# Gate and up projections by seven block products (Strassen's form) in a two-layer streaming encoder trunk on Trainium2

## The reference

```python
D_MODEL = 1024; SEQ = 512; DEC_SEQ = 32; DEPTH = 2; D_FF = 2816

def rms_norm(x, w):
    xf = x.astype(F32)
    y = xf * lax.rsqrt(jnp.mean(xf * xf, axis=-1, keepdims=True) + EPS)
    return (y * w.astype(F32)).astype(x.dtype)

def swiglu(x, w_gu, w_down):
    gate, up = jnp.split(x @ w_gu, 2, axis=-1)
    return (jax.nn.silu(gate) * up) @ w_down

# in trunk(), for every layer l:
    h = h + 0.5 * swiglu(rms_norm(h, p['norm_ffn1'][l]), p['ffn1_w_gu'][l], p['ffn1_w_down'][l])
    ...                                     # mixer
    h = h + 0.5 * swiglu(rms_norm(h, p['norm_ffn2'][l]), p['ffn2_w_gu'][l], p['ffn2_w_down'][l])
```

## Time and profile before

| | us |
|---|---|
| median of 3 runs | 2420.63 |
| lowest, highest | 2418.0, 2421.4 |
| span of the profiled execution | 2420.0 |
| PE busy in it | 2389.0 |
| PEld busy | 2266.8 |
| DVE busy | 1428.3 |
| ACT busy | 940.4 |

### The profile page before, as it was taken

How to read it: one execution, slowest core, us unless ns; L and a number is a source line. 1 busy time by engine, 2 the same in 40 slices (tenths; PEclk the granted TensorE clock), 3 DMA queues, 4 the chain that set the end, 5 groups by cost and what they waited for, 6 DMA issues and landing times.

```text
span 2420.0 us, 48986 instructions
## 1 busy us (share of the span) xinstructions
PE 2389.0 (99%) x19329; PEld 2266.8 (94%) x19329; DVE 1428.3 (59%) x2253; ACT 940.4 (39%) x1369; POOL 13.9 (1%) x50
## 2 busy tenths in 40 slices
PE   9999999999999999999999999999999999999998
PEld 8999999998999999999999999999999989999997
DVE  6553555788577555534555553555788866543554
ACT  4221233576355442222233221224677744221232
POOL 1000000000000000000000000000000000000000
PEclk9999999999999999999999999999999999999999
DMA  5232232332422233322332232332222222232231
GB/s 143 87 109 66 87 100 70 106 115 73 124 69 67 66 94 89 104 79 78 91 91 79 87 111 67 92 92 84 67 77 66 65 72 87 87 113 61 87 102 49
DMA packets 396031, 208.77 MB, mean 86 GB/s; under 512 B 10015, under 2 KB 392086, under 8 KB 395894
## 3 DMA queue, kind: packets, MB, share of 16 engines
q1 hardware_dynamic: 390502, 203.17, 29.2%
q10 hardware_dynamic: 5392, 3.72, 0.5%
HBM read 201.41 MB, written 5.45 MB: 85 GB/s over the span
## 4 chain that ended last, share of the span: by engine, by line
PE 84%; DVE 7%; ACT 4%; DVEq 3%; issue 1%; ACTq 1%; DMA 0%; SPq 0%
PE PD L2054 20%; PE PD L2050 14%; PE PD L2060 14%; PE PD L2061 14%; PE PD L2062 12%; PE PD L2059 2%; PE PD L2056 2%; DVE wlo L1216 1%; DVE c_xl L1745 1%; DVE c_xl L1721 1%; DVEq L1723 1%; DVEq L1731 1%; DVEq L1746 1%; ACT whi L538 0%; PE PM L2467 0%
## 5 line engine op out<-in xcount | busy, mean ns | idle before, releaser
L538 ACT ACTIVATE whi<-raw 128x1024 fp32r<-128x1024 f32 (+4 forms) x348 | 381.2, 1096 | 938.3 <-PE PD L2062 932.6
L2050 PE MATMUL PD<-XB,whi 128*128 128x288 f32 x2008 | 602.6, 300 | 0.4 <-DVE wlo L1216 0.4
L2061 PE MATMUL PD<-XB,wlo 128*128 128x288 f32 x2008 | 591.9, 295 | 0.0
L2060 PE MATMUL PD<-XB,whi 128*128 128x288 f32 x2008 | 591.3, 294 | 0.0
L2062 PE MATMUL PD<-XB,wlo 128*128 128x256 f32 x2008 | 558.8, 278 | 0.0
L2054 PE MATMUL PD<-XB,whi 128*128 128x512 f32 x1392 | 551.5, 396 | 0.5 <-DVE XB L1254 0.5
L2061 PEld LDWEIGHTS PD<-XB,wlo 128*128 128x128 f32 x2008 | 377.7, 188 | 63.8
L2050 PEld LDWEIGHTS PD<-XB,whi 128*128 128x128 f32 x2008 | 376.7, 188 | 3.4 <-DVE wlo L1216 0.8
L2062 PEld LDWEIGHTS PD<-XB,wlo 128*128 128x128 f32 x2008 | 377.8, 188 | 0.0
L2060 PEld LDWEIGHTS PD<-XB,whi 128*128 128x128 f32 x2008 | 377.7, 188 | 0.0
L2054 PE MATMUL PD<-AB,whi 128*128 128x512 f32 x704 | 277.9, 395 | 0.0
(11 more groups left out here) (444 smaller groups left out, 3433.7 us busy)
## 6 DMA issues: line engine op xcount, KB each, us to landing
raw<-in_ffn_w_gu SPq DMA_DIRECT2D x176, 512.0 KB, 3.8
raw<-in_ffn_w_down SPq DMA_DIRECT2D x32, 768.0 KB, 4.8
raw<-in_ab_w_in SPq DMA_DIRECT2D x44, 512.0 KB, 3.9
raw<-in_ffn_w_down SPq DMA_DIRECT2D x32, 640.0 KB, 4.4
raw<-in_c_w_in SPq DMA_DIRECT2D x32, 512.0 KB, 4.1
LM<-cum_rows SPq DMA_DIRECT2D x8, 512.0 KB, 4.8
raw<-in_ab_w_out SPq DMA_DIRECT2D x16, 256.0 KB, 2.9
raw<-in_ab_w_out SPq DMA_DIRECT2D x8, 512.0 KB, 3.7
```

Of the source, the lines that this page charges most:

```text
L538: A(whi[ps % 2][:, 0:k, :], raw[ps % 4][:, 0:k, :], ACT.Copy).then_inc(S["hi_ready"], 1)
L2050: mm(front, hi, x[:, 0, r, 0:FRONT], start=first, stop=False)
L2060: mm(front, hi, x[:, 1, r, 0:FRONT], start=False, stop=False)
L2061: mm(front, lo, x[:, 0, r, 0:FRONT], start=False, stop=final)
```

## The change

In every block two of the 22 hidden tiles (`PLAIN`) stay as they were, with six matmuls a row. For the other 20 (`PAIRS`), gate and up of a hidden tile are computed together. The input features are taken as two halves, 0 to 511 and 512 to 1023, the outputs as gate and up, the tokens as two halves of 272 (front and rear, HT). The eight block products of such a 2 x 2 by 2 x 2 multiplication are replaced by seven of sums (Winograd's form of Strassen). Each of the seven products has 4 rows of three matmuls of 272 columns (`product`).

- *Tokens.* Four sums of token halves are needed: three in XT (4 x 3 x 272, high and low), made by `t_diff`, `t_rest`, `t_lows` on DVE and `t_first`, `t_highs` on ACT for each of four row pairs, and one in place in XB (`t3_highs`, `t3_lows`), when the plain units are over. In blocks 1 and 2 (`spread`; blocks are counted 0 to 3) three of the four row pairs are handled in the last phase before; in blocks 0 and 3 all four are handled within the plain units.
- *Weights.* A tile's gate and up blocks (1 MB, V, two buffers) land by three DMAs. V lies where the four `raw` buffers lie. The first two tiles of a group are loaded when the low parts of the last units in that place are made, later ones when the low parts of the tile two before are made (`pair_low`). DVE makes four sums of blocks (`diffs`, `sums`, `last_sums`) into WS, which lies on part of WL; ACT makes three high parts (`plain_hi` of three landed blocks, `diff_hi` and `sum_hi` of two sums each), DVE the low parts (`plain_lo`, `diff_lo`, `sum_lo`).
- *Results.* Products are accumulated in three PSUM banks per tile. ACT copies partial sums (`p1_copy` after product 1, `u2_copy` after 6, `u3_copy` after 7), products 2, 3 and 4 add to banks, and DVE adds the rest (`up_rear`, `gate_rear`). Product 2 waits for p1_copy; 6 for p1_copy and sum_lo; 7 for u2_copy; 4 for u3_copy; 3 for up_rear and sum_lo; 1 for plain_lo; 5 for diff_lo. RS is now applied to the gate's halves only, and to up after the down product (`scaled_residual`, two instructions instead of two).
- *Groups.* There are three groups of 6, 8 and 8 hidden tiles (the first with the two plain ones), each followed by 8 down units of 6 or 8 rows. Products 4 and 3 of a group's last tile stand within the first down unit, after its row 2. The blocks' loops are written out.

Of the diff, blank lines, the ACT functions not shown and repeats are left out:

```diff
-GROUPS = [(0, 12), (12, 10)]
+GROUPS = [(0, 6), (6, 8), (14, 8)]
+PLAIN = 2
+PAIRS = FT - PLAIN
...
+W_OF = {1: 0, 2: 1, 4: 2, 7: 3, 5: 4, 6: 5, 3: 6}
+BANK_OF = {1: "front", 2: "front", 6: "sum", 7: "sum", 4: "sum", 5: "rear", 3: "rear"}
...
-            def ffn(tag, gu, down, start=0):
+            def ffn(f, gu, down, start=0, order=None):
...
+                for g, nf, ss in groups(f):
+                    f0 = GROUPS[g][0]
+                    u0 = plan[f"{tag}_down{g}"][0]
+                    for s in ss:
+                        b, t = s % 2, PLAIN + s % PAIRS
+                        if s in ss[:2]:
+                            sp.wait_ge(S["lo_ready"], max(u for u in range(u0) if u % 4 // 2 == b) + 1 + CREDIT)
+                        if s >= 2:
+                            sp.wait_ge(S["pair_low"], 3 * (s - 1))
...
+                        if j < 4:
+                            sp.wait_ge(S["pair_low"], 3 * (max(s for s in ss if s % 2 == u % 4 // 2) + 1))
...
+            def p1_copy(s):
+                act.wait_ge(S["product_done"], product_at[s, 1])
+                if s >= 2:
+                    act.wait_ge(S["act_made"], hidden_of(s - 2) + 1)
+                A(bank(s, "sum"), bank(s, "front"), ACT.Copy).then_inc(S["pair_copied"], 1)
...
+            def u3_copy(s):
+                act.wait_ge(S["product_done"], product_at[s, 7])
+                if s:
+                    act.wait_ge(S["c22_made"], s)
+                A(US[:, 1, :], bank(s, "sum"), ACT.Copy).then_inc(S["pair_copied"], 1)
...
+            def t_first(f, r):
+                c = NORM_COL[FFNS[f][1]]
+                act.wait_ge(S["parts_made"], 13 * f + 3 * r + 1)
+                A(TF[:, 0, :], DH[:, :], ACT.Copy, scale=vec[:, c + r:c + r + 1])
+                A(XN[:, :], H[:, r + 4, HT:T], ACT.Copy, scale=nvec[:, c + r + 4:c + r + 5])
+                act.drain().then_inc(S["parts_high"], 1)
+            def t_highs(f, r):
+                act.wait_ge(S["parts_made"], 13 * f + 3 * r + 2)
+                A(XT[:, 0, r, :, :], TF[:, :, :], ACT.Copy).then_inc(S["parts_high"], 1)
...
+            def scaled_residual(m, ps):
+                TT(RT[:, :], line(ps), RS[:, :], ALU.mult)
+                dve.drain().then_inc(S["pair_read"], 1)
+                STT(H[:, m, :], RT[:, :], 0.5, H[:, m, :], ALU.mult, ALU.add)
+                dve.drain()
+            def diffs(s):
+                b = s % 2
+                dve.wait_ge(pair_landed[b], 48 * (s // 2 + 1))
+                if users(s):
+                    dve.wait_ge(S["product_done"], product_at[users(s) - 1, 7])
+                TT(WS[b][:, 0:2, :], V[:, b, 0:3:2, :], V[:, b, 3:4, :].to_broadcast([P, 2, 4 * P]), ALU.subtract)
+                dve.drain().then_inc(S["pair_sums"], 1)
+            def sums(s):
+                b = s % 2
+                TT(WS[b][:, 2, :], WS[b][:, 1, :], V[:, b, 0, :], ALU.add)
...
+            def diff_lo(s):
+                b = s % 2
+                dve.drain()
+                dve.wait_ge(S["pair_high"], 3 * s + 1)
+                TT(WL[b][:, 3:5, :], WS[b][:, 0:2, :], WH[b][:, 3:5, :].bitcast(F), ALU.subtract).then_inc(S["pair_low"], 1)
...
+            def up_rear(s):
+                dve.wait_ge(S["pair_copied"], 3 * s + 3)
+                TT(UR[:, :], bank(s, "rear"), US[:, 1, :], ALU.add).then_inc(S["c22_made"], 1)
+            def gate_rear(s):
+                dst = TG[:, s % 2, HT:T]
+                dve.wait_ge(S["product_done"], product_at[s, 3])
+                TT(dst, bank(s, "rear"), US[:, 0, :], ALU.add)
+                dve.drain()
+                TT(dst, dst, RS[:, HT:T], ALU.mult)
+                dve.drain().then_inc(S["gate_scaled"], 1)
+            def activation(s):
+                k = hidden_of(s)
+                dve.wait_ge(S["silu_done"], k + 1)
+                dve.wait_ge(S["product_done"], product_at[s, 4])
+                dve.wait_ge(S["ah_ready"], k)
+                TT(AV[:, 0:HT], bank(s, "sum"), TG[:, s % 2, 0:HT], ALU.mult)
+                TT(AV[:, HT:T], UR[:, :], TG[:, s % 2, HT:T], ALU.mult)
+                dve.drain().then_inc(S["act_made"], 1)
...
+            def t_diff(r):
+                TT(DH[:, :], H[:, r, 0:HT], H[:, r, HT:T], ALU.subtract)
+                dve.drain().then_inc(S["parts_made"], 1)
+            def t_rest(f, r):
+                c = NORM_COL[FFNS[f][1]]
+                dve.wait_ge(S["parts_high"], 9 * f + 2 * r + 1)
+                STT(TF[:, 1, :], XN[:, :], -1.0, TF[:, 0, :], ALU.mult, ALU.subtract)
+                STT(T3[:, r, :], H[:, r, HT:T], nvec[:, c + r:c + r + 1], XN[:, :], ALU.mult, ALU.add)
+                dve.drain()
+                STT(TF[:, 2, :], H[:, r + 4, 0:HT], vec[:, c + r + 4:c + r + 5], TF[:, 1, :], ALU.mult, ALU.subtract)
+                dve.drain().then_inc(S["parts_made"], 1)
+            def t_lows(f, r):
+                dve.wait_ge(S["parts_high"], 9 * f + 2 * r + 2)
+                TT(XT[:, 1, r, :, :], TF[:, :, :], XT[:, 0, r, :, :].bitcast(F), ALU.subtract)
+                dve.drain().then_inc(S["parts_made"], 1)
...
+            def ffn(f, e, begun=False, order=None, final=False):
+                tag = FFNS[f][0]
+                up0 = plan[f"{tag}_up"][0]
+                spread = f in (1, 2)
+                s0 = PAIRS * f
...
+                for b in range(2 * PLAIN):
+                    k, t = FT * f + b // 2, b // 2
+                    if not spread:
+                        t_diff(b)
+                        t_rest(f, b)
+                        t_lows(f, b)
+                    if b == 2:
+                        diffs(s0)
+                        sums(s0)
+                    if b == 0:
+                        dve.wait_ge(S["rs_ready"], e)
+                    dve.wait_ge(S["unit_done"], up0 + b + 1 + CREDIT)
+                    if b % 2 == 0:
+                        TT(TG[:, t, :], line(up0 + b), RS[:, :], ALU.mult)
+                        dve.drain().then_inc(S["pair_read"], 1)
...
+                    if b == 1:
+                        lo(up0 + 3)
+                    if b == 2:
+                        diff_lo(s0)
+                        last_sums(s0)
+                        plain_lo(s0)
+                        sum_lo(s0)
+                    if b % 2:
+                        act_lo(k, t)
+                for g, nf, ss in groups(f):
+                    s0, last = ss[0], ss[-1]
+                    u0 = plan[f"{tag}_down{g}"][0]
                     if g == 0:
+                        t3_lows(f)
...
+                    diffs(s0 + 1)
+                    sums(s0 + 1)
+                    diff_lo(s0 + 1)
+                    last_sums(s0 + 1)
+                    plain_lo(s0 + 1)
+                    gate_front(s0)
+                    sum_lo(s0 + 1)
+                    for s in ss:
+                        if s > s0:
+                            activation(s - 1)
+                        if s + 2 <= last:
+                            diffs(s + 2)
+                            sums(s + 2)
+                        up_rear(s)
+                        if s + 2 <= last:
+                            diff_lo(s + 2)
+                        else:
+                            lo(u0 + s + 1 - last)
+                        if s > s0:
+                            act_lo(hidden_of(s - 1), slot_of(s - 1))
+                        if s < last:
+                            gate_front(s + 1)
+                        gate_rear(s)
+                        if s + 2 <= last:
+                            last_sums(s + 2)
+                            plain_lo(s + 2)
+                            sum_lo(s + 2)
+                    activation(last)
+                    act_lo(hidden_of(last), slot_of(last))
...
+                        if j == KT - 2 and not closing:
+                            diffs(last + 1)
+                            sums(last + 1)
+                            diff_lo(last + 1)
+                            last_sums(last + 1)
+                            plain_lo(last + 1)
+                        if j == KT - 1 and not closing:
+                            sum_lo(last + 1)
...
+            def product(s, p):
+                b, w, out = s % 2, W_OF[p], bank(s, BANK_OF[p])
+                if p <= 3:
+                    k0, t0 = ((0, 0), (4, 0), (4, HT))[p - 1]
+                    moving = XB[:, :, k0:k0 + 4, t0:t0 + HT]
+                elif p == 7:
+                    moving = XB[:, :, 0:4, HT:T]
+                else:
+                    moving = XT[:, :, :, {5: 0, 6: 1, 4: 2}[p], :]
+                opens = p in (1, 5)
+                for q in range(4):
+                    hi, lo = WH[b][:, w, q * P:(q + 1) * P], WL[b][:, w, q * P:(q + 1) * P]
+                    mm(out, hi, moving[:, 0, q, :], start=q == 0 and opens, stop=False, skip_group_check=not opens)
+                    mm(out, hi, moving[:, 1, q, :], start=False, stop=False, skip_group_check=not opens)
```

(29 more changed lines are left out.)

571 lines of the change are left out of this document (371 added, 200 removed).

## The result

| | us |
|---|---|
| before, median of 4 runs beside it | 2420.88 |
| changed, median of 4 runs (2447.95 to 2451.34) | 2449.36 |
| ratio, 95% interval | 1.0119 (1.0105 to 1.0134) |
| span of the profiled execution, changed | 2446.2 |
| forecast (range) | 2431 (2409 to 2454) |

The change makes the kernel 1.2% slower. The forecast had 0.4%: right in sign, and the time lies within the range, but by the medians 28 us were lost and not 10. Span against span, 26.2 us were lost where the sum had 10 (2430 against 2420.0).

A forecast was written before the change was run, and what follows sets the result against it. PE, busy 99% of 2420.0 us, was taken as the bound. New waits of 121 us against 119.6 gained gave +1; restarts +5 and overheads +4 made 2430, as a median 2431 us (range 2409 to 2454).

The forecast's parts named there:

- What bounds, and what is removed: PE sets the pace at about 0.458 ns a column; seven products in 80 tiles save 119.6 us.
- cutting them in six costs nothing: Down rows, cut into six matmuls, stay as many and take no extra time.
- (c): Openings of the blocks, with block 1's closing units: PE waits for token sums, evacuations and pair work, 67 us in all.
- VectorE per tile: In steady tiles DVE needs 10.3 us against PE's 10.46, so PE sets the pace with 0.16 us spare.
- The 4 us for overheads: Drains, waits and straight-line code in DVE's 13 steps a tile: between 0 and about +9, taken as +4 us.
- Rival B: DVE is the bound of every tile, through over 0.16 us of unseen time per tile: 2450 us, chance 0.12.
- (a): Entry to each block's second and third group: product 1 and the second tile wait, 43 us in all.
- (b): Exits of groups: the last hidden tile's chain outlasts PE's rows in the down unit, 11 us in all.
- rival C: PE's clock halves after long waits in the program's middle, +10 to +20 us: 2440 us, chance 0.11.
- restarts and overheads: Some 68 PE restarts after waits at 0.08 us each, +5 us, and DVE overheads within tiles, +4 us.

The follow-up runs named there:

- e5_groups_only: Kernel before, with only the three groups of 6, 8 and 8 hidden tiles and six-matmul rows, no block products: 2424.9 us (1.0018).
- e4: Changed kernel with gate_front's multiplication done twice on DVE in each tile, first into a spare tile: 2449.8 us (1.0117).
- e11_fill_valid: Changed kernel with unread 272-column matmuls filling some 85% of PE's long waits, every sum left as it was: 2442.8 us (1.0091).
- e7_slots_entry: Changed kernel with landing buffers counted from each block's first unit, and later groups' first pair begun one down unit earlier: 2415.1 us (0.9976).
- e10_evacuate_first: e7_slots_entry with openings reordered, first HGRN head loads waiting only for their own buffers, first plain unit evacuated once the root mean square is there: 2396.2 us (0.9898).

## Why the prediction fell short

**What bounds, and what is removed.** Right in kind: PE's rate sets a steady tile. The price was off: a tile takes 10.54 us in all four blocks, not 10.46, so 80 tiles give 113.6 us, **6 less**. The step that failed is "about 0.458 ns a column, whatever the cut", and with it "cutting them in six costs nothing". The plain rows, and some 560 of the 704 down rows, take 0.753 us in the changed kernel (here 55 rows in 41.43), where the rows before took 0.748 and 0.7465: **some 4 more** in the down rows, and 0.7 in the plain ones, which the table below has within (c).

```profile
240.96 0.29 PE L2403 MATMUL PD<-AB,whi 128*128 128x288 f32 x1
...
282.39 0.30 PE L2403 MATMUL PD<-AB,whi 128*128 128x288 f32 x1
```

The prediction rested on two cuts in the earlier trace rows that differ by 3 ns a row, in the direction of the error; I had called it nothing. That the cut itself makes the difference isn't shown: the down rows of the first group, with the same cut, take 0.747 us in three of the blocks, and e5_groups_only has both prices too. The cause of the dearer stretches stays open.

**VectorE per tile.** The sum of 10.3 was right (10.26 by e4). The 4 us for overheads were not there: the tiles are PE's, and DVE catches up. Rival B is out by e4.

**(a) Entries.** Forecast 5.8 and 3.1, in the first block 3.6 and 2.1. Start to start product 1 waits 5.8 to 6.1 and 3.0 to 3.1 us in blocks 1 to 3, and 3.6 and 2.0 in the first: right, step by step. The second tiles lose 14.8 us in sum for 10.4: with the waits filled (e11_fill_valid) nearly all lose the 1.3 us of the forecast, so the rest is the slow clock's. **(b) Exits:** at the six-row ones 1.2 us ahead of the last tile's row and 0.6 within it, 1.9 as forecast. But in the last block I missed that the first down block lands in the last tile's half: 2.8 and 1.1 us at the ends of its second and third group, **some 4**. I had used the unit numbers modulo four for the entries and not asked the same of the exits.

**(c) Openings.** First block: 7.37, 5.55 and 3.00 us; up to product 1 it loses 14.9 us for a forecast 15.0. Last: 6.51 at product 1, forecast 6.6. Blocks 1 and 2 lost more: the third unit waited 3.46 for a forecast 2.0, product 1 2.02 for 3.6, and the slow clock lay between; from the mean square to product 1 it is 24.1 and 23.8 us where four plain units left 16.6 before, so 7.5 and 7.2 for 5.6: **3 to 4**. And a term is missing: the token sums for block 1 are made in the GLA output units, which lose 3.4 us, PE waiting for low parts; I had put 3 at block 1's closing units (3.7) and nothing there.

**The clock.** I put rival C beside the forecast at 0.11 instead of into it, with waits of 4 to 7 us already in my sum. My "the granted clock is 1.00 everywhere but at the end" was a wrong reading, and so was "no row inside the program tests it": two stretches of the kernel before read 0.50 behind waits of 1.9 and 2.7 us. The mechanism came: granted clock 0.51 behind an entry. PE's idle time grew by 94 instead of 121 us, and its busy time is 2321.5 instead of 2275, in part because slow work took the place of waiting. Its net price by e11_fill_valid is **4 to 7 us**, below my +10 to +20; a reader of the changed profile alone would put it at 20.

**The sum.** All rows are start to start, changed against before, in us:

| | forecast | measured |
|---|---|---|
| 80 tiles by seven products | -119.6 | -113.6 |
| down rows | 0 | +3.9 |
| (a) product 1 at the entries | 32.4 | 32.5 |
| (a) second tiles behind them | 10.4 | 14.8 |
| (b) exits | 10.8 | 14.5 |
| (c) openings, up to product 1 | 39.7 | 43.6 |
| (c) openings, behind it | 24.6 | 26.6 |
| (c) closing units ahead of blocks 1 and 2 | 3.0 | 7.1 |
| restarts and overheads | 9 | within the rows above |
| rest of the program | 0 | -2.6 |
| sum | 10 | 27 (by the spans 26.2) |

The price of PE's work is the largest single error, 10 us; the waits came out 18 longer in many places, of which the slow clock has 4 to 7 and the missed landing some 4. No wait was wrong by much, but waits of 121 us against a gain of 120 left nothing for small terms of one sign. The sign was in part luck: gain and waits alone gave +1, and what made the forecast "slower" were 9 us for restarts and overheads, 4 of which weren't there. The page of the Trainium skill on TensorE ("TensorE: Matmul & The Clock Gate", "Back-to-back issue gap") has a fixed price for each matmul, which I had set aside as its total didn't agree with the rows. The rows of e5_groups_only don't bear such a price out either: six matmuls of 1632 columns take 0.747 us in its third group, as five did before.

## What to carry to other kernels

When a change trades PE's work for waits on an engine that becomes full, the gain and the new waits are both large and the difference is small: price each wait by its chain, then look for what starts the chain, since e7_slots_entry and e10_evacuate_first turned +1.2% into -1.0% with the same arithmetic in another order and with other landing buffers. Slow clock after a wait costs only where no later wait for the same chain takes it up; look at idle and busy time together before blaming it, and look for it in windows behind every long wait of the kernel before, not in the page's digits. Read the price of an engine's work in several stretches of the program: a difference of 0.8% in it cost 10 us here, as much as the whole forecast. And ask of each buffer that is shared by position (unit number modulo four) what lies in it at *every* place of the program, ends of groups included.
